# Delta heads: the block inverse in 32-wide quarters with z's projection between its levels, decay distances and four grams moved ahead

## The chip, the cores and the metric

One NeuronCore of a Trainium2 chip runs the whole program. The metric is device time in microseconds of that core for one execution. Engines are named as the profile names them: PE (TensorE; PEld are its weight loads), DVE (VectorE), ACT (ScalarE), POOL (GpSimd), SP (SyncE, which starts DMAs).

## What is computed

The reference is one inference step of a decoder layer: a feed-forward half, differential attention beside a gated DeltaNet branch, a merge, and a second feed-forward half, for 1024 prompt tokens and 32 sample tokens (8 sequences of 4). The change lies in the DeltaNet branch, which per head (8 heads, 128 wide) projects q, k, v and z, convolves and normalizes q, k, v, and then, in chunks, does

```python
decay = jnp.exp(jnp.where(incl, gc[..., :, None] - gc[..., None, :], -jnp.inf))
lower = jnp.where(strict, jnp.einsum('bhncd,bhnmd->bhncm', kb, k) * decay, 0.0)
sol = lax.linalg.triangular_solve(jnp.eye(C) + lower, rhs, left_side=True, lower=True)
qk = jnp.einsum('bhncd,bhnmd->bhncm', q, k) * decay
def step(S, inp):
    v_new = u_i - w_i @ S
    o_i = qd_i @ S + qk_i @ v_new
    S = S * gt_i + kd_i.T @ v_new
o = rmsnorm(o) * silu(z)
```

The kernel computes it with chunks of 128 tokens (8 tiles of the prompt and one of 32 sample rows) and forms the inverse of (I + lower) itself.

## The kernel before

`delta_heads` (L1129) runs eight heads one after another; heads 1 to 5 are a hardware loop (`Fori(1, H - 2)`), the others are written out (`schedule`, L1252). Each engine has its own list of instructions, written by hand, in `head(h)`; they meet only through semaphores (`wait_ge`, `then_inc`), and an engine that waits holds everything behind it in its list. Nothing reorders the lists.

**A projection piece** (`piece`, L1945) is 24 products of 128x128 weights with 352 token columns (8 slices of the 1024 inputs, each as high x high, high x low and low x high parts); c = 0, 1, 2 are the three thirds of the 1056 tokens, and `piece(h, kind, c, i, of)` does part i of `of` of one. Two PSUM banks take turns for them; `take` on ACT empties one. Weights come in by SP (`load`), ACT makes the high part (`high`), DVE the low part (`low`).

**PE's list of a head** (L2018): the last v piece of the head before, with the turns of q and k into token rows (`token`) and the gated output rows of the head before (`out_rows`); q pieces 0 and 1; `grams(0)`, `grams(1)` (products of k with q and k for two tiles each, L2052); q piece 2; `grams(2)`, `grams(3)`; z piece 0, a third of z piece 1, `grams(4)` (the sample tile), the rest of z; then the inverse; then `value_rows`, `key_products`, and the loop over the eight tiles with the state (`fill` puts k and v projections of the next head between the steps).

**The inverse** is built by doubling: the diagonal blocks of size s are inverted, the next level joins pairs of them. For each level 1 to 6 there are, for x = 0, 1 (tiles 0 to 3 and 4 to 7): P = masked lower x U on PE (`pmul`, L2072, into bank 4 + x), a copy to SBUF on ACT (`moves`, L1499), R = turned U x P (`rmul`, L2089, into bank 6 + x), U - R on DVE (`update`, L1767), and the turned U for the next level (`turned`, L1782: DVE turns 32x32 blocks, which suffices below level 6; `tmul` on PE turns the 64-wide blocks at level 6). POOL makes the masked lower for each level (`mask`, L1892). All products of levels 1 to 5 are of whole 128x128 tiles; level 6 is 64x64. Between levels 1, 2, 3 PE does three small steps for the 32 sample rows (L2119, L2122, L2126).

**What feeds it.** The cumulated decay of the head lies in `lo_t` (SP's `load_gc`). DVE makes the distances -|gc_i - gc_j| into `qk_t` (`distances`, L1707, L1709), ACT their exponent into `lo_t` (L1486), POOL the triangle into `qk_t` (L1875, L1877), DVE then multiplies with the grams (`products`, L1717, L1719), POOL masks. POOL's list in a head: kp (L1872), the triangles, the decayed q (L1879, L1881), the masks of level 0, the sample masks (L1903), level 1, kd (L1908), levels 2 to 6, km (L1911).

f32 products appear in the profile as two passes each, a MATMUL and a LDWEIGHTS row for both; the projection's f32r products as one.

Of the kernel before, what the change touches and what calls it, by code (L numbers as in the profile page):

```python
# [7 lines left out]
ALU = mybir.AluOpType  # L8
# [7 lines left out]
P = 128  # L16
# [23 lines left out]
LEVELS = 7  # L40

# [4 lines left out]
C_LEV = C_CAUS + P  # L46
C_ONE = C_LEV + LEVELS * P
# [13 lines left out]
def shape_constants():  # L61
# [6 lines left out]
    for n in range(LEVELS):  # L68
        s = 1 << n
        same = i[:, None] // (2 * s) == i[None, :] // (2 * s)  # L70
        c[:, C_LEV + n * P:C_LEV + (n + 1) * P] = same & (i[:, None] // s % 2 == 1) & (i[None, :] // s % 2 == 0)
# [1057 lines left out]
def delta_heads(nc, m, w_in, w_next, gc_dram, oa_hi_dram, oa_lo_dram, oa_dram, o_dram, state, conv_prompt, conv_sample, delta_prompt, delta_sample):  # L1129
# [6 lines left out]
    with ExitStack() as ctx:  # L1136
# [18 lines left out]

        mask_s, p_mm_s, p_moved_s, t_mm_s, t_moved_s, r_mm_s, u_done_s = (
# [38 lines left out]
        mk = sb("mk", [P, 2, 4, P])  # L1195
        uu = sb("uu", [P, NT, P])
        with ExitStack() as early:
            s_hi, s_lo = (early.enter_context(nc.sbuf_tensor("dl_rows_" + n, [P, H * NS], F32R)) for n in ("hi", "lo"))
        tt = sb("tt", [P, 2, 4, P])
# [5 lines left out]

        ssq = sb("ssq", [P, 4, NT, 2])
# [3 lines left out]
        pp = sb("pp", [P, 2, 4, P])  # L1210
        km = tt[0:NS, :, :, :].rearrange("p a b d -> p (a b) d")
        vn = sb("vn", [P, 2, P])

# [31 lines left out]
        def sample_cols(a):  # L1245

            return a[:, SX:SX + NB * 7].rearrange("p (b w) -> p b w", w=7)

# [43 lines left out]
        def _(sp):  # L1292
# [64 lines left out]
        def _(act):  # L1357
# [83 lines left out]
            def head(h):  # L1441
# [36 lines left out]
                take(h, "q", 0)  # L1478
                take(h, "q", 1)
# [3 lines left out]
                for x in range(3):  # L1483
# [3 lines left out]
                    if x == 0:  # L1487
                        take(h, "q", 2)
# [4 lines left out]
                for c in range(3):  # L1493
                    take(h, "z", c, weights=False)

                def moves(i, x, n):

                    act.wait_ge(p_mm, 12 * h + i + 1)
                    nc.scalar.copy(pp[0:n, x, :, 0:n], bank4(4 + x, 4, n)).then_inc(p_moved, 1)  # L1499
                    if n < P:  # L1500
# [3 lines left out]
                for lev in range(1, LEVELS):  # L1504
                    for x in range(2):
                        moves(2 * (lev - 1) + x, x, P if lev < LAST else P // 2)
                    if lev == 1:
                        n, k = unit(h, "z")
                        if exists(n + 2):
                            high(n + 2, k)  # L1510
                    if lev == 2:
                        act.wait_ge(t_mm_s, h + 1)
                        act.wait_ge(p_mm_s, 2 * h + 2)
                        nc.scalar.copy(pp_s[:, :], m.ps[0:NS, 0, XS:XS + NS]).then_inc(p_moved_s, 1)
# [2612 lines left out]
```

## Time and profile before

| | |
|---|---|
| median of 3 runs | 3486.53 us (3486.32 to 3491.23) |
| profiled execution | 3496.3 us, span 3494.6 us, granted clock 0.99 |
| PE / PEld busy | 3383.1 us (97%) / 3224.6 us (92%) |
| DVE / ACT / POOL busy | 1975.2 us (57%) / 1469.0 us (42%) / 791.7 us (23%) |
| the eight delta heads | 98.7 us each |

Times in the views are us from the span's start. Matmuls are pipelined and their ends are modelled, so the distance between the starts of two of them says more than the length of one; a merged row xN runs from the first start to the last end. The granted clock is that of PE, as a share of 2.4 GHz.

### The profile page before, as it was taken

What the parts mean: (1) busy time and instruction counts of PE and PEld (TensorE: products, weight loads), DVE (VectorE), ACT (ScalarE), POOL (GpSimd) and SP (SyncE); (2) the same over time, 40 slices, a digit from 0 to 9 for tenths busy, and PEclk for the clock granted to TensorE, in tenths of its full rate; (3) what the DMA queues carried; (4) which work ended last, traced back from release to release, by engine and by line L of the source; (5) the groups of instructions that cost most, each with busy time, mean ns of one, the idle gap of its engine ahead of it and who ended that gap; (6) DMA issues with size and microseconds to landing.
All of it is one profiled execution on the core that took longest, in us unless ns stands there. A gap on an engine that the chain in (4) does not pass through costs nothing. (4 is left out here: it accounts for less than half of the span.)

```text
span 3494.6 us, 64138 instructions
## 1 busy us (share of the span) xinstructions
PE 3383.1 (97%) x24746; PEld 3224.6 (92%) x24746; DVE 1975.2 (57%) x3332; ACT 1469.0 (42%) x2993; POOL 791.7 (23%) x644
## 2 busy tenths in 40 slices
PE   7999999999999999898999999999999999999998
PEld 7999999998888888776999999999999899999998
DVE  6655566754555455543566566666341765556555
ACT  5322234545555455433444343444322732223444
POOL 3232210102222221000232334444001332331000
PEclk9999999999999999999999999999999999999999
DMA  4232246732222222499111111114432322224664
GB/s 163 77 87 76 74 153 200 231 107 75 68 68 68 69 68 70 161 356 336 35 51 51 45 38 41 44 45 137 137 99 68 122 76 77 81 82 130 209 191 142
DMA packets 351845, 384.66 MB, mean 110 GB/s; under 512 B 22492, under 2 KB 259110, under 8 KB 351422
## 3 DMA queue, kind: packets, MB, share of 16 engines
q1 hardware_dynamic: 341606, 347.78, 31.7%
q0 software_dynamic: 9888, 32.88, 2.7%
q8 instruction: 179, 2.93, 0.4%
q14 instruction: 88, 0.72, 0.1%
q10 hardware_dynamic: 84, 0.35, 0.0%
HBM read 305.53 MB, written 75.40 MB: 109 GB/s over the span
## 5 line engine op out<-in xcount | busy, mean ns | idle before, releaser
L670 PE MATMUL ps<-p_hi,w_hi 128*128 128x352 f32 x912 | 304.6, 334 | 3.0 <-PEq L120 1.5
L670 PE MATMUL ps<-p_hi,w_lo 128*128 128x352 f32 x912 | 293.7, 322 | 0.0
L670 PE MATMUL ps<-p_lo,w_hi 128*128 128x352 f32 x912 | 293.1, 321 | 0.0
L1960 PE MATMUL ps<-p_hi,w_hi 128*128 128x352 f32 x840 | 281.5, 335 | 3.8 <-DMA p_lo<-d_oa_lo 3.8
L1960 PE MATMUL ps<-p_hi,w_lo 128*128 128x352 f32 x840 | 277.1, 330 | 0.0
L1960 PE MATMUL ps<-p_lo,w_hi 128*128 128x352 f32 x840 | 276.5, 329 | 0.0
L670 PEld LDWEIGHTS ps<-p_hi,w_hi 128*128 128x128 f32 x912 | 172.1, 189 | 5.1 <-issue 1.9
L2773 PE MATMUL ps<-op_hid_hi,w_hi 128*128 128x384 f32 (+1 forms) x528 | 170.9, 324 | 2.7 <-ACT plain L3710 1.7
L2773 PE MATMUL ps<-f_hid_hi,w_hi 128*128 128x352 f32 x528 | 171.3, 324 | 1.5 <-DVE w_lo L2448 1.4
L670 PEld LDWEIGHTS ps<-p_lo,w_hi 128*128 128x128 f32 x912 | 172.5, 189 | 0.0
L670 PEld LDWEIGHTS ps<-p_hi,w_lo 128*128 128x128 f32 x912 | 171.6, 188 | 0.0
L2773 PE MATMUL ps<-f_hid_lo,w_hi 128*128 128x352 f32 x528 | 169.8, 322 | 0.0
L2773 PE MATMUL ps<-f_hid_hi,w_lo 128*128 128x352 f32 x528 | 169.7, 321 | 0.0
L2773 PE MATMUL ps<-op_hid_hi,w_lo 128*128 128x384 f32 (+1 forms) x528 | 169.3, 321 | 0.0
L2773 PE MATMUL ps<-op_hid_lo,w_hi 128*128 128x384 f32 (+1 forms) x528 | 169.3, 321 | 0.0
L1960 PEld LDWEIGHTS ps<-p_hi,w_hi 128*128 128x128 f32 x840 | 159.9, 190 | 5.1 <-issue 3.8
L1960 PEld LDWEIGHTS ps<-p_hi,w_lo 128*128 128x128 f32 x840 | 159.9, 190 | 0.7
L1960 PEld LDWEIGHTS ps<-p_lo,w_hi 128*128 128x128 f32 x840 | 160.1, 191 | 0.5
L1892 POOL TENSOR_TENSOR dl_mk<-dl_lo_t,cst 128x512 f32<-128x512 f32 x112 | 140.9, 1275 | 49.1 <-PE ps L2081 43.1
L2448 DVE TENSOR_TENSOR w_lo<-w_raw,w_hi 128x512 fp32r<-128x512 f32 x136 | 100.5, 746 | 86.6 <-ACT w_hi L2444 86.4
L411 ACT ACTIVATE at_prob<-ps,at_nmax 128x256 f32<-128x256 f32 (+7 forms) x128 | 94.4, 739 | 81.2 <-DVE at_nmax L517 79.5
L2444 ACT CAST w_hi<-w_raw 128x512 fp32r<-128x512 f32 x136 | 83.8, 620 | 105.8 <-PE ps L2773 105.7
(686 smaller groups left out, 10691.6 us busy)
## 6 DMA issues: line engine op xcount, KB each, us to landing
w_raw<-in_ffn_w_out_dram SPq DMA_DIRECT2D x136, 256.0 KB, 3.3
w_raw<-in_w_in_dram SPq DMA_DIRECT2D x67, 512.0 KB, 4.0
sa_v<-in_cache_v_dram SPq DMA_DIRECT2D x120, 256.0 KB, 6.5
w_raw<-in_ffn_w_in_dram SPq DMA_DIRECT2D x48, 512.0 KB, 5.1
sa_k<-in_cache_k_dram SPq DMA_DIRECT2D x72, 256.0 KB, 5.5
f_s<-in_ffn_w_out_dram SPq DMA_DIRECT2D x64, 256.0 KB, 3.3
pair_s<-in_ffn_w_out_dram SPq DMA_DIRECT2D x64, 256.0 KB, 3.2
d_hid<-f_gb SPq DMA_DIRECT2D x44, 264.0 KB, 2.2
```

What stands on the lines that cost most here:

```text
L411: nc.scalar.activation(pr[:, i % 2, a, 0:(i + 1) * P], m.ps[:, 2 + 2 * a:4 + 2 * a, :].rearrange("p b k -> p (b k)")[:, 0:(i + 1) * P], AC ...
L670: mm = nc.tensor.matmul(m.ps[:, bank, 0:CH], a[:, k, w], b[:, f, cols(c)], start=(f == 0 and i == 0), stop=(f == KT - 1 and i == 2))
L1892: nc.gpsimd.tensor_tensor(mk[:, x, :, :], lo_t[:, 4 * x:4 * x + 4, :], msk, ALU.mult).then_inc(mask_done, 1)
L1960: mm = nc.tensor.matmul(m.ps[:, (k + c) % 2, 0:CH], a[:, k, f * P:(f + 1) * P], x[:, f, cols(c)], start=(j == 0), stop=(j == len(terms) - 1))
L2444: nc.scalar.copy(unit_slot(u, False), unit_raw(u)).then_inc(e.out_hi, 1)
L2448: nc.vector.tensor_tensor(unit_slot(u, True), unit_raw(u), unit_slot(u, False).bitcast(F32), ALU.subtract).then_inc(e.out_lo, 1)
L2773: mm = nc.tensor.matmul(m.ps[:, bank, 0:hi - lo], unit_slot(u, low_part)[:, o * P:(o + 1) * P], y[:, k, 0:hi - lo], start=(k == 0 and n == ...
```

## The change

1. Levels 1 to 5 work on 32x32 blocks on the diagonal. POOL cuts the four diagonal blocks of each tile out of `lo_t` into `lo_d` (4 copies of 32 partitions for each x) and makes the masks of levels 0 to 4 at once (`diagonal`). U is kept as `uc` (128 x 32 for each tile). A level is, for each tile and each of four blocks b, one 32x32 product with 32 columns from rows 32b in quarter b. Level 5 joins pairs of blocks straight from `lo_t` (two products for each tile and step). POOL puts the blocks back into the wide `uu` (`put`); level 6 reads `lo_t` itself instead of a mask. `uu` is zeroed once at the start.
2. The last two z pieces are cut into twelve parts of four products, one behind each P and each R step of levels 1 to 5 and two within level 6.
3. On PE, grams(0) to (3) stand ahead of q piece 1, grams(4) ahead of q piece 2.
4. On DVE, `distances` go ahead of the sums and gate rows; ACT takes q's pieces after the exponents; POOL makes kp, decayed q and kd after the masks. SP's `load_gc` waits for p_mm instead of mask_done.
5. Small steps use banks 2 and 3; ACT takes z pieces 1 and 2 behind level 4 and at the end.

The core of the diff:

```diff
-                wait(sp, mask_done, 14 * x)
+                wait(sp, p_mm, 12 * x)
...
                 nc.vector.tensor_scalar(col[:, :, :], m.cols[:, bass.ds(h, 1), :, :].rearrange("p o k t -> p (o k) t"), 1.0, None, ALU.mult).then_inc(staged, 1)
+                dve.wait_ge(staged, h + 1)
+                distances(0)
                 sums(0)
+                distances(1)
+                distances(2)
                 if inner:
...
                 def update(lev, x):
-                    n = P if lev < LAST else P // 2
+                    n = P // 2
+                    tiles = slice(4 * x, 4 * x + 4)
                     dve.wait_ge(r_mm, 12 * h + 2 * (lev - 1) + x + 1)
                     dve.wait_ge(u_done, 14 * h + 2 * (lev - 1) + x + 1)
-                    u = uu[0:n, 4 * x:4 * x + 4, P - n:P]
-                    nc.vector.tensor_tensor(u, u, bank4(6 + x, 4, n), ALU.subtract).then_inc(u_done, 1)
+                    if lev < LAST - 1:
+                        nc.vector.tensor_tensor(uc[:, tiles, :], uc[:, tiles, :], sub4(6 + x), ALU.subtract).then_inc(u_done, 1)
+                    elif lev == LAST - 1:
+                        if isinstance(h, int) and h == 0:
+                            dve.wait_ge(u_zero, 1)
+                        nc.vector.tensor_scalar(uu[0:SUB, tiles, SUB:n], sub4(6 + x)[0:SUB], -1.0, None, ALU.mult)
+                        nc.vector.tensor_scalar(uu[n:n + SUB, tiles, n + SUB:P], sub4(6 + x)[n:n + SUB], -1.0, None, ALU.mult).then_inc(u_done, 1)
+                    else:
+                        nc.vector.tensor_scalar(uu[0:n, tiles, n:P], bank4(6 + x, 4, n), -1.0, None, ALU.mult).then_inc(u_done, 1)
...
+                def diagonal(x):
+                    tiles = slice(4 * x, 4 * x + 4)
+                    pool.wait_ge(low_done, NT * h + 4 * x + 4)
+                    if x == 0:
+                        wait(pool, r_mm, 12 * h)
+                        pool.wait_ge(tri_done, 3 * h + 3)
+                    else:
+                        pool.wait_ge(mask_done, 4 * h + 2)
+                        wait(pool, u_turned, NTURN * h)
+                    pool.nop(nofuse=True)
+                    for b in range(4):
+                        rows = slice(SUB * b, SUB * b + SUB)
+                        nc.gpsimd.tensor_copy(lo_d[rows, tiles, :], lo_t[rows, tiles, rows]).then_inc(cut_done, 1)
+                    pool.wait_ge(cut_done, 8 * h + 4 * x + 4)
+                    first = m.cst[:, C_LEV:C_LEV + SUB].rearrange("p (o d) -> p o d", o=1).to_broadcast([P, 4, SUB])
+                    nc.gpsimd.tensor_tensor(mk[:, x, 0, :, :], lo_d[:, tiles, :], first, ALU.mult).then_inc(mask_done, 1)
+                    k = LEVELS - 3
+                    more_levels = m.cst[:, C_LEV + SUB:C_LEV + SUB + k * SUB].rearrange("p (l o d) -> p l o d", l=k, o=1).to_broadcast([P, k, 4, SUB])
+                    again = lo_d[:, tiles, :].rearrange("p (o t) d -> p o t d", o=1).to_broadcast([P, k, 4, SUB])
+                    nc.gpsimd.tensor_tensor(mk[:, x, 1:1 + k, :, :], again, more_levels, ALU.mult).then_inc(mask_done, 1)
+                def put(x):
+                    tiles = slice(4 * x, 4 * x + 4)
+                    pool.wait_ge(u_done, 14 * h + 2 * (LAST - 2) + x + 1)
+                    if isinstance(h, int) and h == 0 and x == 0:
+                        pool.wait_ge(u_zero, 1)
+                    pool.nop(nofuse=True)
+                    for b in range(4):
+                        rows = slice(SUB * b, SUB * b + SUB)
+                        nc.gpsimd.tensor_copy(uu[rows, tiles, rows], uc[rows, tiles, :]).then_inc(put_done, 1)
...
+                diagonal(0)
+                diagonal(1)
...
+                put(0)
+                put(1)
...
                 piece(h, "q", 0)
-                piece(h, "q", 1)
                 grams(0)
                 grams(1)
-                piece(h, "q", 2)
                 grams(2)
                 grams(3)
+                piece(h, "q", 1)
+                grams(4)
+                piece(h, "q", 2)
                 piece(h, "z", 0)
-                piece(h, "z", 1, 0, 3)
-                grams(4)
-                def pmul(lev, x, n):
-                    pe.wait_ge(mask_done, 14 * h + 2 * lev + x + 1)
...
+                def p_products(lev, x):
+                    if lev == 1:
+                        pe.wait_ge(mask_done, 4 * h + 2 * x + 2)
+                    pe.wait_ge(u_done, 14 * h + 2 * (lev - 1) + x + 1)
+                    if lev > 1:
+                        pe.wait_ge(p_moved, 12 * h + 2 * (lev - 2) + x + 1)
+                    pe.nop(nofuse=True)
                     for j in range(4):
-                        if n < P:
-                            mm = nc.tensor.matmul(m.ps[0:n, 4 + x, j * P:j * P + n], mk[n:P, x, j, 0:n],
-                                                  uu[n:P, 4 * x + j, n:P], start=True, stop=True)
+                        t, out = 4 * x + j, slice(SUB * j, SUB * j + SUB)
+                        if lev < LAST - 1:
+                            for b in range(4):
+                                mm = nc.tensor.matmul(m.ps[rows(b), 4 + x, out], mk[rows(b), x, lev, j, :], uc[rows(b), t, :], start=True, stop=True)
                         else:
-                            mm = nc.tensor.matmul(m.ps[:, 4 + x, j * P:(j + 1) * P], mk[:, x, j, :], uu[:, 4 * x + j, :], start=True, stop=True)
+                            for b in (0, 2):
+                                mm = nc.tensor.matmul(m.ps[rows(b), 4 + x, out], lo_t[rows(b + 1), t, rows(b)], uc[rows(b + 1), t, :], start=True, stop=True)
                     mm.then_inc(p_mm, 1)
...
+                def r_products(lev, x):
+                    pe.wait_ge(p_moved, 12 * h + 2 * (lev - 1) + x + 1)
+                    pe.wait_ge(u_turned, NTURN * h + 2 * (lev - 1) + x + 1)
+                    pe.nop(nofuse=True)
+                    for j in range(4):
+                        t, out = 4 * x + j, slice(SUB * j, SUB * j + SUB)
+                        for b in (range(4) if lev < LAST - 1 else (0, 2)):
+                            mm = nc.tensor.matmul(m.ps[rows(b), 6 + x, out], ttc[rows(b), t, :], ppc[rows(b), t, :], start=True, stop=True)
+                    mm.then_inc(r_mm, 1)
...
+                def p_last(x):
+                    n = P // 2
+                    pe.wait_ge(u_done, 14 * h + 2 * (LAST - 1) + x + 1)
+                    pe.wait_ge(p_moved, 12 * h + 2 * (LAST - 2) + x + 1)
+                    pe.wait_ge(put_done, 8 * h + 4 * x + 4)
...
+                def between(k):
+                    piece(h, "z", 1 + k // 6, k % 6, 6)
+                for lev in range(1, LAST):
                     for x in range(2):
-                        pe.wait_ge(u_done, 14 * h + 2 * (lev - 1) + x + 1)
-                        if lev > 1:
-                            pe.wait_ge(p_moved, 12 * h + 2 * (lev - 2) + x + 1)
-                        pmul(lev, x, n)
-                        if lev == LAST:
-                            tmul(x, n)
+                        p_products(lev, x)
+                    between(2 * lev - 2)
                     for x in range(2):
-                        rmul(lev, x, n)
+                        r_products(lev, x)
                     if lev == 1:
...
+                    between(2 * lev - 1)
+                pe.wait_ge(u_done_s, 2 * h + 2)
+                p_last(0)
+                p_last(1)
+                between(10)
+                between(11)
+                r_last(0)
+                r_last(1)
+                pe.wait_ge(taken, 3 * unit(h, "z")[0] + 3)
```

## Rows read from the trace of the kernel before

**Rows 1.** An inner head: length, busy us of PE, PEld, DVE, ACT, POOL, then clock, DMA.

```profile
1895.57:1994.28 98.71, 97.45 (x685) 93.17 (x684) 61.75 (x106) 41.19 (x106) 36.81 (x29) 0.97 0.15 44
```

**Rows 2.** Timeline of PE, the inverse: start, us, engine, line, operation, [idle before].

```profile
1930.02 1.95 PE L2081 MATMUL ps<-dl_uu,dl_mk 128*128 128x128 f32 x16
...
1934.71 2.39 PE L2081 MATMUL ps<-dl_uu,dl_mk 128*128 128x128 f32 x16 [0.70 <-POOL dl_mk L1892]
...
1951.23 0.65 PE L2078 MATMUL ps<-dl_uu,dl_mk 64*64 64x64 f32 x8
...
1954.25 1.76 PE L2138 MATMUL ps<-cst,dl_cs 128*128 128x128 f32 x8
```

**Rows 3.** Timeline of PE: passes on 32 columns, sample attention and a small step.

```profile
1493.69 1.06 PE L1079 MATMUL ps<-vals,w_raw 128*32 128x128 f32 x32
...
1496.77 0.24 PE L1051 MATMUL ps<-k_s,sa_q_zeroed 128*32 128x32 f32 x8
...
1939.06 0.24 PE L2123 MATMUL ps<-dl_uu,dl_mk_s 32*32 32x32 f32 x2
```

**Rows 4.** Groups of PE by line and shape: busy us, mean ns of one.

```profile
L1079 PE MATMUL ps<-vals,w_raw 128*32 128x128 f32 x64 | 2.0, 274 | 0.0
...
L1051 PE MATMUL ps<-k_s,sa_q_zeroed 128*32 128x32 f32 x8 | 0.2, 194 | 0.0
...
L2078 PE MATMUL ps<-dl_uu,dl_mk 64*64 64x64 f32 x16 | 1.3, 222 | 0.1
```

**Rows 5.** Timeline of PE, a change of tile shape and back.

```profile
1922.93 0.32 PE L1960 MATMUL ps<-p_hi,w_hi 128*128 128x352 f32 x1
1923.09 0.32 PE L1960 MATMUL ps<-p_lo,w_hi 128*128 128x352 f32 x1
1923.33 0.30 PE L2052 MATMUL ps<-dl_css 128*32 128x64 f32 x2
1923.56 0.43 PE L1960 MATMUL ps<-p_hi,w_lo 128*128 128x352 f32 x1
```

**Rows 6.** Timeline of ACT, the copy of a level.

```profile
1931.11 0.59 ACT L1499 COPY dl_pp<-ps 128x512 f32<-128x512 f32 x1 [0.43 <-PE ps L2081]
```

**Rows 7.** Timeline of DVE, distances and products.

```profile
1908.56 2.60 DVE L1707 TENSOR_TENSOR dl_qk_t<-dl_lo_t,dl_col 128x512 f32<-128x512 f32 x1
...
1911.81 0.68 DVE L1707 TENSOR_TENSOR dl_qk_t<-dl_lo_t,dl_col 128x512 f32<-128x512 f32 x1
...
1917.19 0.35 DVE L1717 SCALAR_TENSOR_TENSOR dl_lo_t<-ps,dl_sc,dl_lo_t 128x128 f32<-128x128 f32 x1
...
1917.65 0.34 DVE L1717 SCALAR_TENSOR_TENSOR dl_lo_t<-ps,dl_sc,dl_lo_t 128x128 f32<-128x128 f32 x1
```

**Rows 8.** Timeline of ACT, the exponents.

```profile
1911.53 1.28 ACT L1481 ACT_TABLE_LOAD   x1
...
1914.02 0.63 ACT L1486 ACTIVATE dl_lo_t<-dl_qk_t 128x512 f32<-128x512 f32 x1
```

**Rows 9.** Timeline of POOL, triangles and a mask.

```profile
1914.72 2.16 POOL L1875 TENSOR_TENSOR dl_qk_t<-dl_lo_t,cst 128x512 f32<-128x512 f32 x1 [4.11 <-ACT dl_lo_t L1486]
...
1919.92 1.29 POOL L1877 TENSOR_TENSOR dl_qk_t<-dl_lo_t,cst 32x32 f32<-32x32 f32 x1
...
1927.11 1.28 POOL L1892 TENSOR_TENSOR dl_mk<-dl_lo_t,cst 128x512 f32<-128x512 f32 x1
```

**Rows 10.** Timeline of POOL, a copy of 32 partitions in attention.

```profile
903.81 0.28 POOL L600 COPY v_s<-at_v_rows 32x128 f32<-32x128 f32 x1 [7.25 <-DVE at_o_lo L561]
```

**Rows 11.** Busy times of one stretch, columns as in rows 1.

```profile
1964.70:1968.20 3.50, 3.50 (x15) 3.50 (x15) 0.10 (x1) 0.27 (x1) 0.00 (x0) 0.51 0.00 0
```

**Rows 12.** Timeline of PE ahead of that stretch and in it.

```profile
1961.61 1.85 PE L2200 MATMUL ps<-dl_wq,dl_sts 128*128 128x8 f32 x16
...
1965.22 0.49 PE L1960 MATMUL ps<-p_hi,w_lo 128*128 128x352 f32 x1
1965.51 0.49 PE L1960 MATMUL ps<-p_hi,w_hi 128*128 128x352 f32 x1
```

More of the change, by code:

```diff
@@ L1486, in head @@
                     nc.scalar.activation(lo_t[0:n, 4 * x:4 * x + k, 0:n], qk_t[0:n, 4 * x:4 * x + k, 0:n], ACT.Exp).then_inc(decay_done, 1)
-                    if x == 0:
-                        take(h, "q", 2)
+                for c in range(3):
+                    take(h, "q", c)
                 if not more:
@@ L1492, in head, with moves @@
                     nc.scalar.activation(zs[:, :], xc[:, 0, 0:T], ACT.Silu).then_inc(z_silu, 1)
[L1493 to L1499, printed above, removed]
-                    if n < P:
+                take(h, "z", 0, weights=False)
+                def moves(lev, x):
+                    act.wait_ge(p_mm, 12 * h + 2 * (lev - 1) + x + 1)
+                    if lev < LAST:
+                        nc.scalar.copy(ppc[:, 4 * x:4 * x + 4, :], sub4(4 + x)).then_inc(p_moved, 1)
+                    else:
+                        n = P // 2
+                        nc.scalar.copy(pp[:, x, :, :], bank4(4 + x, 4, n)).then_inc(p_moved, 1)
                         act.wait_ge(t_mm, 2 * h + x + 1)
@@ L1737, in head @@
                 low(n, k)
-                if not more:
-                    row_low(0)
-                    row_low(1)
-                for x in range(3):
-                    distances(x)
-                    if x == 1:
-                        gather(h, 2)
-                        product(h, 2, 1)
-                if not more:
-                    row_low(2)
+                gather(h, 2)
+                product(h, 2, 1)
                 for t in range(NT):
                     products(t)
-                    if t == 3:
-                        product(h, 2, 2)
+                    if not more and t == 3:
+                        row_low(0)
+                if not more:
+                    row_low(1)
                 def base(x):
@@ new lines, in head @@
+                diagonal(0)
+                diagonal(1)
+                pool.wait_ge(low_done, NT * h + NT)
+                wait(pool, p_mm_s, 2 * h)
+                for i in range(2):
+                    nc.gpsimd.tensor_tensor(mk_s[:, i, :], lo_t[0:NS, TT, 0:NS], m.cst[0:NS, C_LEV + i * SUB:C_LEV + i * SUB + NS], ALU.mult).then_inc(mask_s, 1)
+                pool.wait_ge(scales, 4 * h + 4)
+                nc.gpsimd.tensor_tensor(kp[:, :, :], tok[:, :, 1, :], by_scale(BPE), ALU.mult).then_inc(kp_done, 1)
@@ new lines, in p_last @@
+                def p_last(x):
+                    n = P // 2
+                    pe.wait_ge(u_done, 14 * h + 2 * (LAST - 1) + x + 1)
+                    pe.wait_ge(p_moved, 12 * h + 2 * (LAST - 2) + x + 1)
+                    pe.wait_ge(put_done, 8 * h + 4 * x + 4)
+                    pe.nop(nofuse=True)
+                    for j in range(4):
+                        mm = nc.tensor.matmul(m.ps[0:n, 4 + x, j * P:j * P + n], lo_t[n:P, 4 * x + j, 0:n], uu[n:P, 4 * x + j, n:P], start=True, stop=True)
+                    mm.then_inc(p_mm, 1)
```

132 lines of the change are left out of this document (60 added, 72 removed).

## Prediction

> **What bounds the kernel now.** I read the page first. Section 1, engines by busy time, has PE far ahead of DVE. So what counts is how long PE needs for its own list and where it waits. The slices show the granted clock at nine tenths or more throughout. Next, the busy times by stretch: in one inner head of the delta loop (1895.57 to 1994.28, 98.71 us; eight such heads in the kernel) PE is busy for 97.45 us, DVE for 61.75, POOL for 36.81 [rows 1]. An edit that only shifts work to another engine brings nothing here; one that shortens PE's list brings it nearly whole.
>
> Then PE's timeline of that head. The levels of the inverse run as one block, with no other product between them. L2081 (P) and L2097 (R) alternate, 16 passes each, the first P at 1930.02, the second at 1934.71, five pairs, until the last level's 64-wide products start at 1951.23 and value_rows at 1954.25 [rows 2]. Levels 1 to 5 take 21.2 us, level 6 takes 3.0, together 24.2 us. A phase of 16 passes is about 1.95 us with its last pass's 0.28, so some 0.11 a pass. PE's 0.70 us of waiting ahead of level 2 is put down to POOL's mask [rows 2]. The z projection stands ahead of the block, where it hides the chain that feeds the first mask.
>
> **Packing, levels 1 to 5.** A phase of 16 full passes (two for each of 8 tiles) becomes 64 passes of 32x32 with 32 columns in levels 1 to 4, and 32 passes in level 5: 576 passes a head in place of 160. What they cost depends on whether quarters run side by side. The trace has each half of this: L1079 uses four column quarters, and 32 passes of 128 columns fill 1.06 us of which one pass is 0.27, so 0.79/31 = 0.025 us a pass, against the 0.11 of the whole array; L1051, with 32 columns, has eight passes in 0.24 us where one is 0.194, so they start 0.007 apart [rows 3, 4]. With the last pass of a group, four side by side, costing what one costs, I need the pitch of one quarter: 64x64 passes with 64 columns fill 0.65 us by eights, one being 0.222, so 0.061 apart [rows 2, 4]; half the columns, near 0.028. The four starts of a group at 0.007 come to 0.028 too. A tile, two passes in each of four quarters, is then 0.056 us and a phase 8 x 0.056 = 0.45 us. Upper bound of the overlapped case: passes of one quarter lie 0.045 apart (L2123: two 32x32 passes in 0.24 us [rows 3], one of them as long as L1051's), a phase 0.75 us. I take 0.45, since the eight of L2078 show that passes behind the first come closer.
>
> **The change of shape.** The z pieces put whole-array products on either side of each phase, so PE changes tile shape twice. L1960 to the 32-column L2052 is 1923.09 to 1923.33, 0.24 us against the 0.16 from one L1960 to the next, so +0.08; back, the two passes of L2052 and the way to L1960 take 0.23 together, some +0.12 [rows 5]. A phase costs 0.45 + 0.08 + 0.12 = 0.65 us, ten of them 6.5. The three small 32x32 steps behind levels 1 to 3 stay, now within the same shape: 0.3 together. Levels 1 to 5: 6.8 us in place of 21.2. Level 6 keeps its matrices; it gets two pieces in the middle, one more pair of shape changes and a small one at its start: 3.0 + 0.3 = 3.3 us. The block is 10.1 us in place of 24.2: **14.1 us less a head**.
>
> **Is the chain within a level covered?** Between P and R, and between R and the next P, stands a piece of four z products, 4 x 0.16 = 0.64 us, with the two changes of shape 0.85 or so. P to R: ACT starts 0.3 us after P's last start, and each copy has a quarter of the columns: I estimate half of L1499's 0.59 or less [rows 6], two of them 0.6. R of tiles 0 to 3 needs the first only. R to P: DVE's update shrinks in the same way, two are 0.6 to 0.7; the turns shrink too and are wanted only by the next R. About 0.85 us against 0.85: covered, with little to spare; if it isn't, 0.2 us at ten places is 2 us a head. ACT's silus stand behind the copies of level 5, ahead of those of level 6, as now; PE then has an R, a piece and a P to do. POOL's masks, which the 0.70 us waited for, are made ahead of level 1, so that wait goes.
>
> **The work moved ahead.** z's last two thirds (48 x 0.16 = 7.7 us) no longer hide what comes before the first P. Without waits PE would come there at 1930.02 - 7.7 = 1922.3. I follow the feeding chain, head start unchanged. DVE now starts distances(0) at 1908.56 and is at distances(1) at 1911.81; L1707 takes 2.60 us for the first beside POOL's kp, 0.68 alone [rows 7]. Moved ahead of the sums, with kp behind the masks, the three cost 3.1 us in place of 5.1, part of it in gaps where DVE waits for ACT's squares. So the sums end near 1908.2, scales, low, gather and one product near 1913.3. ACT's exponentials now need the root ahead of them, and that the last sums: table load at 1908.5, and as now 3.1 us from it (1911.53) to the end of the first decay (1914.02 + 0.63) [rows 8]: 1911.6. POOL's triangle product, 1.28 alone for this shape (L1892) to 2.16 beside DVE, gives 1913.0 to 1913.9 [rows 9]. DVE's products, 0.46 us a tile (1917.19 to 1917.65) [rows 7], begin then. PE: q0 (24 x 0.16) to 1907.0, four grams 3.1 and q1 3.85, so 1913.9; grams(4), now ahead of q2, wait for the first two tiles' products, 1914.9: **a new wait of about 1 us**, with q2 and z0 queued behind it. DVE ends tile 7 at 1917.7. POOL's diagonal(0) needs tile 3 (1915.8) and triangle three: four copies at 0.28 (L600 copies 32x128 in that), a mask at 0.4, one at 1.28; twice, 5.6 to 6 us in all, ends near 1922 [rows 9, 10]. PE arrives at 1923.3. So P waits 0 to 1 us. One of DVE's 1080-column products lies between the two turns, on the way of the second half. New waits together 0.6 to 2.6 us, taken 1.6: **12.5 us less a head**. kp, q and kd behind the masks on POOL, three operations of 1024 or 1152 columns, each under 3.2 us at L1892's rate of 0.0025 a column and its start, end by 1932; put needs level 4, which ends near 1934, copies 2 x 1.1, and p_last comes at 1937: free. take(z,2) runs under r_last. Behind put on POOL wait km and the DMAs of the tails, not wanted before the states. SP's load_gc waits for p_last's products instead of the last mask; only the next head's loads queue behind it, and lo_t is wanted at the next distances, the whole state loop later.
>
> **The sum.** 8 x 12.5 = 100 us. The profiled execution is 3496.3 us (span 3494.6), 9.8 above the median of the runs; it gives 3396, the median 3486.5 gives **3386**. Own range of this case: new waits 0.6 instead of 1.6, and one late fall of the clock less a head in three, 3486.5 - 8 x 13.6 - 6 = 3372, less 10 for a stage that is shorter than its rows add up to: 3362; phases of 0.75 us (3.0 a head) and waits of 2.6, 3486.5 - 8 x 8.5 = 3418.
>
> **Rivals.** (1) *The quarters come in turn.* No row has passes that differ in both row and column quarter and write the same bank. If they start one behind another, 0.028 apart, a phase of 64 is 1.8 us: 8 x 1.35 + 2 x 0.45 = 11.7 back of 12.5, hence 3480. Where they do overlap but PE can't be fed faster than the 0.025 us a pass that L1079 sustains (the 0.007 of L1051 is a burst of eight), a phase of 64 is 1.6 us and of 32 0.8: 8 x 1.15 + 2 x 0.35 = 9.9 back, 3466. Middle 3473.
> The Trainium skill speaks against the change here: TensorEngine Tiling (Array Packing), Restrictions and Gotchas, says that different row tiles can't use one PSUM bank at the same time. Here all four write bank 4 + x or 6 + x, though in different partitions. TensorE: Matmul & The Clock Gate, section "Wait — 56ns, not 53.3ns?", gives about 62 ns for a MATMUL when the sequencer's firmware decodes it; 288 x 62 would be 17.9 us a head and the time 3494, an estimate from that page. L1079's 16 products (32 passes) in 1.06 us are 0.05 to 0.07 each and refute neither.
> (2) *Slower: in turn, with the load exposed, and the clock falls.* At 0.045 a pass 576 passes are 25.9 us against 4.5, 21.4 back of 12.5: 8.9 us worse a head, 3558. The turning point is (4.5 + 12.5)/576 = 0.030 us a pass. An emptier array brings the other part: from 1964.7 to 1968.2, behind an array fed little by 16 passes of 8 columns, the granted clock is 0.51, the level of 1.2 GHz, and L1960 starts every 0.29 us instead of 0.16 [rows 11, 12]. If all twelve pieces ran so, +6.2 us a head. In the forecast nearly half of each level is z at full width, so I expect no more falls than now.
> (3) *POOL is late.* L1877, a 32x32 operation, took 1.29 us beside DVE's convolution [rows 9]. At that price diagonal ends 8 us later and the eight copies of put bind too: some 2.6 us left of 12.5, 3466.
> (4) *No change*: rival 1 at its worst, or two of these in part.
>
> **Chances.** Forecast 0.70, rival 1 0.10 (a fifth of it within the bound of no change), rival 2 0.10, rival 3 0.05, rival 4 0.05. The range takes in the first, rival 3 and most of rival 1: 3362 to 3478. About 0.2%, 7 us, is what a measurement of this kernel can tell from none. Faster 0.83, same 0.07, slower 0.10.
>
> **What would show it.** Right: P and R phases of 64 passes with 0.45 us from first to last start; PE waits ahead of grams(4) and of the first P of 0 to 2 us, none elsewhere in the block; ten pieces of four z products; p_last some 14 us behind the first P; a head near 86 us; clock 0.97 or more. Wrong: phases of 1.8 us (rival 1), 3 us with a clock near 0.5 (rival 2), or PE waiting for POOL's dl_mk or dl_uu by microseconds (rival 3).

## The result and the profile after

| | before | after |
|---|---|---|
| median of 20 runs each, same chip | 3491.88 us (3486.32 to 3501.72) | 3483.47 us (3476.24 to 3492.07) |
| ratio after / before, 95% interval | | 0.9972 (0.9964 to 0.9979) |
| profiled execution, span | 3494.6 us | 3478.1 us |

One run after, of 12249.86 us at a granted clock of 0.57, is left out of the range and of the ratio.

The change makes the kernel 0.28% faster, about 8 us (the two profiled executions happen to lie 16.5 us apart). The prediction was 3386 us, with 3478 as its upper end: of the 100 us forecast nine tenths are missing.

The page of the kernel after, engines by busy time and the instruction queue (packets, MB, share):

```profile
span 3478.1 us, 70910 instructions
...
PE 3326.4 (96%) x28074; PEld 3147.3 (90%) x28074; DVE 1932.1 (56%) x3348; ACT 1440.9 (41%) x2993; POOL 700.9 (20%) x693
...
q8 instruction: 236, 3.87, 0.5%
```

PE's busy time fell by 57 us (from 3383.1), but the span by 16.5 only. The other 40 us are idle time of PE that was not there before. The waits of PE in the delta stage (1690 to 2400) name it; the columns are us in total, times, longest:

```profile
PE ps L2131 <- DVE dl_uc L1779: 34.7, 7, 5.1
PE ps L2004 <- issue: 9.3, 5, 2.5
PE ps L2131 <- DVE dl_uc L1770: 2.9, 6, 0.6
```

L2131 is P, L2145 is R, L2004 is the projection's product (L1960 before), L1779 is DVE's update, L1770 the base. Seven times PE stands 5 us ahead of level 2's P. The timelines of DVE and POOL in one head show why; they answer to [rows 7] and [rows 9]:

```profile
1918.62 0.31 DVE L1770 STREAM_TRANSPOSE dl_uc<-dl_ttc 128x128 f32<-128x128 f32 x1
1918.86 7.84 DVE L1608 SCALAR_TENSOR_TENSOR dl_cs<-dl_xc,conv_weight,dl_cs 128x1080 f32<-128x1080 f32 x1
1926.62 0.47 DVE L1779 TENSOR_TENSOR dl_uc<-dl_uc,ps 128x128 f32<-128x128 f32 x2
...
1918.87 2.10 POOL L1939 TENSOR_TENSOR dl_kp<-dl_tok,dl_sc 128x1152 f32<-128x1152 f32 x1
1920.94 2.34 POOL L1941 TENSOR_TENSOR dl_q_t<-dl_q_t,dl_cs 128x1024 f32<-128x1024 f32 x1
1923.24 0.24 POOL L1943 TENSOR_TENSOR dl_wq<-dl_q_t,dl_css 128x32 f32<-128x32 f32 x1
1923.45 2.10 POOL L1948 TENSOR_TENSOR dl_kd<-dl_tok,dl_col 128x1152 f32<-128x1152 f32 x1
```

`product(h, 2, 3)`, a convolution product of 1080 columns, and kp start within 0.01 us of each other. The product ends 7.84 us later, 1.15 us after the last of POOL's four operations; by itself it takes 1.33 us (e2 below). It takes 7.83 to 7.85 us in all eight heads. Level 1's update is queued behind it on DVE. PE's timeline of the same head, against [rows 2], and the busy times of the stretch behind (length, PE, PEld, DVE, ACT, POOL, clock, DMA):

```profile
1918.17 0.45 PE L2131 MATMUL ps<-dl_uc,dl_mk 32*32 32x32 f32 x32
1919.08 0.45 PE L2131 MATMUL ps<-dl_uc,dl_mk 32*32 32x32 f32 x32 [0.45 <-DVE dl_uc L1770]
...
1920.30 0.86 PE L2145 MATMUL ps<-dl_lo_d,dl_ttc 32*32 32x32 f32 x64
...
1927.04 1.08 PE L2131 MATMUL ps<-dl_uc,dl_mk 32*32 32x32 f32 x64 [4.91 <-DVE dl_uc L1779]
...
1936.62 0.77 PE L2131 MATMUL ps<-dl_uc,dl_mk 32*32 32x32 f32 x64
...
1928.00:1934.80 6.80, 6.80 (x154) 5.44 (x143) 0.99 (x4) 1.07 (x6) 0.00 (x0) 0.51 0.01 2
```

Behind the 4.91 us the granted clock is 0.51, the level of 1.2 GHz, for about 10 us in nearly every head; before, the stage had seven falls, each of 3.4 us.

For the rest I measured each head between first passes on PE's timeline, the mean of heads 1 to 5. T is the first token transpose, P the first P of the block, V the first of value_rows (before, P to V is the block of 24.2 us and the 7.7 us of z pieces ahead of it that are now inside). V to T is the stretch that leads into the head, from the V of the head before:

| us | T to P | P to V | V to T | head |
|---|---|---|---|---|
| before | 25.6 | 31.9 | 39.3 | 96.8 |
| predicted change | +1.6 | -14.1 | 0 | -12.5 |
| after | 25.6 | 29.4 | 41.3 | 96.3 |
| e1 | 25.9 | 24.4 | 40.4 | 90.8 |
| e2 | 26.0 | 23.9 | 40.1 | 89.9 |
| e6 | 26.3 | 23.8 | 39.3 | 89.3 |
| e7 | 26.3 | 20.0 | 39.0 | 85.3 |
| e8 | 34.0 | 22.1 | 40.9 | 96.9 |
| e9 | 26.3 | 26.3 | 40.0 | 92.6 |
| e10 | 25.6 | 24.3 | 43.4 | 93.3 |

The table ahead of the change gives 98.7 us for each of the eight heads before. That is the length of two of the heads 1 to 5; the other three take 95.5, and the two longer ones hold two falls of the clock of 3.4 us each.

### The profile page after: what moved, and what is told of

The parts are those of the page before. It is cut to its first block and busy times, and to the rows that moved or that the text cites. A ratio compares the mean times of both kernels' runs of the same rounds, so it can differ in the third digit from the quotient of the medians.

```text
span 3478.1 us, 70910 instructions
## 1 busy us (share of the span) xinstructions
PE 3326.4 (96%) x28074; PEld 3147.3 (90%) x28074; DVE 1932.1 (56%) x3348; ACT 1440.9 (41%) x2993; POOL 700.9 (20%) x693
## 5 line engine op out<-in xcount | busy, mean ns | idle before, releaser
L673 PE MATMUL ps<-p_hi,w_hi 128*128 128x352 f32 x912 | 304.8, 334 | 2.6 <-PEq L123 1.4
L2004 PE MATMUL ps<-p_hi,w_hi 128*128 128x352 f32 x840 | 290.7, 346 | 9.1 <-issue 9.0
L673 PE MATMUL ps<-p_hi,w_lo 128*128 128x352 f32 x912 | 293.6, 322 | 0.0
L673 PE MATMUL ps<-p_lo,w_hi 128*128 128x352 f32 x912 | 293.2, 321 | 0.0
L2004 PE MATMUL ps<-p_lo,w_hi 128*128 128x352 f32 x840 | 286.6, 341 | 0.0
L2004 PE MATMUL ps<-p_hi,w_lo 128*128 128x352 f32 x840 | 286.2, 341 | 0.2 <-issue 0.2
L2004 PEld LDWEIGHTS ps<-p_hi,w_hi 128*128 128x128 f32 x840 | 164.8, 196 | 12.5 <-issue 9.8
L2004 PEld LDWEIGHTS ps<-p_lo,w_hi 128*128 128x128 f32 x840 | 164.9, 196 | 2.1
L2004 PEld LDWEIGHTS ps<-p_hi,w_lo 128*128 128x128 f32 x840 | 165.1, 197 | 1.8 <-issue 0.5
L1608 DVE SCALAR_TENSOR_TENSOR dl_cs<-dl_xc,conv_weight,dl_cs 128x1080 f32<-128x1080 f32 x72 | 153.9, 2138 | 4.4 <-DVE dl_cs L1603 2.1
```

The costliest lines, as they stand in the source:

```text
L673: mm = nc.tensor.matmul(m.ps[:, bank, 0:CH], a[:, k, w], b[:, f, cols(c)], start=(f == 0 and i == 0), stop=(f == KT - 1 and i == 2))
L1608: nc.vector.scalar_tensor_tensor(out=cs[:, u, 0:CO], in0=xc[:, u, i:i + CO], scalar=wgt[:, i:i + 1], in1=cs[:, u, 0:CO], op0=ALU.mult, op1 ...
L2004: mm = nc.tensor.matmul(m.ps[:, (k + c) % 2, 0:CH], a[:, k, f * P:(f + 1) * P], x[:, f, cols(c)], start=(j == 0), stop=(j == len(terms) - 1))
```

## The experiments

**e1, the product later.** Takes the convolution product off the way of level 1's update.

```
                 base(1)
-                product(h, 2, 3)
...
                     if lev == 3:
+                        product(h, 2, 3)
                         dve.wait_ge(r_mm_s, h + 1)
```

> The changed kernel with one step of DVE's list moved: the last product of v's convolution, product(h, 2, 3), from ahead of level 1's update to behind level 3's turns. Theory A (POOL's kp, q, kd, four operations back to back, hold up this SBUF-only DVE operation, 7.84 us instead of 1.34; level 1's update stands behind it in DVE's list, and PE waits 4.9 us and then runs 10 us at a clock of 0.5): the wait ahead of level 2 falls to under 0.5 us, the clock inside the block stays at 1.0, a head goes from 96 to about 88.5 us, the time to 3420 to 3430. Rival B (the sparse array of the 32x32 passes is what lowers the clock): the wait goes, but PE still runs at 0.5 for some 10 us of each block, a head near 91.5, the time near 3450. Rival C (another wait takes its place, the copies or updates within a level being late): waits of 0.3 us or more at several phases, the time above 3455.

Measured: 3450.78 us, ratio 0.9889 (0.9868 to 0.9909). Level 2's wait is gone from the waits of PE. In its place stand, in the same view, many short ones without a named releaser:

```profile
PE ps L2004 <- issue: 13.7, 10, 2.5
PE ps L2145 <- issue: 9.4, 17, 1.0
```

Of theory A the wait and the clock came true: between P and V the granted clock is 1.00 in heads 1 to 5, where the changed kernel has 0.78 to 0.88. So rival B is out, though the time is the one that it named. The time missed theory A's 3420 to 3430 us by 20. No theory had the idle time without a releaser, which grew from 9.8 us in the changed kernel to 25.3.

**e2, POOL waits.** The other side of the same collision: the order on DVE stays, POOL starts kp only when the product is done.

```
                 pool.wait_ge(scales, 4 * h + 4)
+                pool.wait_ge(conv_done, 12 * h + 12)
                 nc.gpsimd.tensor_tensor(kp[:, :, :], ...)
```

> The changed kernel with DVE's list as it is; only POOL waits ahead of kp until that last product is done (a wait on conv_done). Theory A: the product takes 1.34 us again, PE's wait ahead of level 2 is under 0.5 us, and kp, q, kd end 1.5 us later than now, which nobody waits for: the time within 0.2% of e1_product_later, 3420 to 3430. If it was the place of the product in DVE's list and not POOL's operations beside it that made it long, it stays at 7.8 us and the time at 3480.

Measured: 3439.62 us, ratio 0.986 (0.9839 to 0.988). DVE's timeline has the same two operations as above:

```profile
1906.17 1.33 DVE L1608 SCALAR_TENSOR_TENSOR dl_cs<-dl_xc,conv_weight,dl_cs 128x1080 f32<-128x1080 f32 x1
1908.25 0.67 DVE L1779 TENSOR_TENSOR dl_uc<-dl_uc,ps 128x128 f32<-128x128 f32 x2 [0.75 <-PE ps L2146]
```

One line on POOL, with no operation added, moved between engines or left out, takes some 40 us off the changed kernel (0.9972 less 0.986, of 3491 us, is 39; the medians say 44). It is the concurrence of the two that cost, not the work of either: in e1 and e2 both are still done. The time is 10 us above the range expected; idle time without a releaser is 21.9 us here.

**e3 and e4, written out.** The changed kernel's PE stands 2.0 to 2.5 us at four head boundaries, each time at the loop's jump back, and at none of the boundaries outside the loop:

```profile
1987.70 0.42 PE L2004 MATMUL ps<-p_hi,w_hi 128*128 128x352 f32 x1 [2.03 <-issue]
```

e3 is e1 with heads 1 to 5 one after another; e4 does the same to the kernel before.

```
-            with eng.Fori(1, H - 2) as h:
+            for h in range(1, H - 1):
                 head(h)
-            head(H - 2)
             head(H - 1)
```

> e1_product_later with heads 1 to 5 written out instead of the hardware loop, nothing else. Theory D (the 2.0 to 2.5 us PE stands still at four of the head boundaries, and not at the others, belong to the loop's jump back: PE's part of the body has grown and its instructions are not there in time): these four gaps go, 9 us less than e1_product_later. Rival (the gaps are a data wait at a head's start): they stay, the same time as e1_product_later.

> The kernel before with heads 1 to 5 written out. Its trace has no gap at the jump back, so theory D expects no change, within 0.2%; if writing out is worth something by itself, here too, it shows as the same 9 us.

Measured: e3 3447.3 us (3435.96 to 3448.35), 3.5 under e1 with overlapping intervals; e4 3493.8, ratio 1.0007 (0.9995 to 1.0019). The gaps at the jump are gone in e3, and the kernel before never had them. The time hardly follows: in V to T, where the gap lay, a fall of the clock of 3.4 us takes its place in two of e3's heads 1 to 5 and in four of e6's (39.6 us from V to T there, 38.0 where there is neither gap nor fall). e3's profiled execution, span 3434.3 us, is at the low end of its runs.

**e6, both repairs.** e2's line and e3's heads.

> Both repairs: GpSimd waits for the head's last convolution product before kp, q and kd (as in e2_pool_waits), and heads 1 to 5 are written out one after another instead of looping (as in e3_written_out). Theory: the two costs lie in different places, so they add. The loop's jump back left TensorE idle 2.2 to 2.6 us at four head boundaries in e2's trace, 9 us in all; off e2's 3439.6 us that is about 3431 us, 3424 to 3436, ratio to the kernel before about 0.983. Rival: the idle time at the jump is not lost but taken up elsewhere (instruction supply is limited as a whole, and e3's median was only 3.5 us under e1's), then it stays at 3437 to 3442 us with more short idle stretches inside the levels.

Measured: 3438.69 us, ratio 0.985 (0.9834 to 0.9867): the rival of that expectation. Against e2 nothing is gained. PE's timeline of one head, P and R of levels 1 to 4:

```profile
1907.44 0.75 PE L2145 MATMUL ps<-dl_lo_d,dl_ttc 32*32 32x32 f32 x64
1909.64 0.75 PE L2131 MATMUL ps<-dl_uc,dl_mk 32*32 32x32 f32 x64 [0.30 <-issue]
1911.15 0.70 PE L2145 MATMUL ps<-dl_lo_d,dl_ttc 32*32 32x32 f32 x58
1913.17 0.26 PE L2145 MATMUL ps<-dl_lo_d,dl_ttc 32*32 32x32 f32 x6 [1.31 <-issue]
1914.27 0.75 PE L2131 MATMUL ps<-dl_uc,dl_mk 32*32 32x32 f32 x64
1915.80 0.60 PE L2145 MATMUL ps<-dl_lo_d,dl_ttc 32*32 32x32 f32 x46
1917.45 0.37 PE L2145 MATMUL ps<-dl_lo_d,dl_ttc 32*32 32x32 f32 x18 [1.05 <-issue]
```

A pause in the middle of a phase, behind its 58th or 46th pass, can be no semaphore: the waits stand ahead of its first and its 33rd pass. I counted PE's passes from one such pause to the next, in e3, e6 and e8: where two follow closely it is 125 or 126 nearly every time. The next three runs ask what that is.

**e7, half the products.** Two of the four blocks of each tile.

```
-                            for b in range(4):
+                            for b in (0, 2):
...
-                        for b in (range(4) if lev < LAST - 1 else (0, 2)):
+                        for b in (0, 2):
```

> e6 with two of the four blocks of 32 left out of each tile in levels 1 to 4, so 32 passes a phase instead of 64; half of the inverse's small levels is not computed. Theory that the passes are limited by their issue (about 0.009 us each, whichever quarter they go to, and with it the supply of instructions): a phase falls from 0.58 to about 0.29 us, eight phases of the four levels give 2.3 us a head, and the short idle stretches without a wait (about 2 us a head in e2's and e3's traces) mostly go as well: 25 to 35 us less than e6, about 3400 us. Theory that each quarter of the array is the limit (16 passes one after another in each of four): a phase stays at 0.55 to 0.6 us, and the time stays within 5 us of e6. Theory that the chain through ScalarE and VectorE sets the pace of a level: phases get shorter, but idle time with a named wait (ScalarE's copy, VectorE's update) takes their place, and the time falls by under 10 us.

Measured: 3418.97 us, ratio 0.9789 (0.9773 to 0.9806), 20 under e6. The kernel leaves out half of the work of levels 1 to 4, so it only tells of time. The waits without a releaser in the blocks of all heads fall from 18.6 us (L2145 9.3, L2131 8.9, level 5's 0.4) to 2.0. In the profiled execution the last head loses again: P to V at a granted clock of 0.56 takes 38.4 us, against 32.1 at 0.79 in e6. But a phase of 32 passes is no half of one of 64:

```profile
1907.59 0.69 PE L2131 MATMUL ps<-dl_uc,dl_mk 32*32 32x32 f32 x32
1909.05 0.69 PE L2145 MATMUL ps<-dl_lo_d,dl_ttc 32*32 32x32 f32 x32
```

With the last pass's 0.19 that is 0.50 us from first to last start, against 0.75 - 0.19 = 0.56 for 64. So a phase is set by the 16 passes of one quarter, about 0.03 us each, and most of the saving is the pauses: the first theory had the pauses right and the second the phase. The page also gives the size of a transfer: e7 has 65537 instructions and 211 packets on q8, e6 69633 and 227. That is 4096 instructions for 16 packets, 256 in one, four to a product (a load and a matmul for either pass). 125 to 126 passes with their loads, 250 to 252 instructions, are then about one packet.

**e8, z ahead.** The pieces leave the levels.

```
                 piece(h, "z", 0)
+                piece(h, "z", 1)
+                piece(h, "z", 2)
...
                 def between(k):
-                    piece(h, "z", 1 + k // 6, k % 6, 6)
+                    return
```

> e6 with z's parts 1 and 2 whole ahead of the levels instead of in twelve pieces between their phases: TensorE has nothing to do between the phases. Theory: the pieces hide the chain product, copy, product, update, turn of each level. Exposed, a level costs two phases of 0.6 us and the chain's 1.5 to 2 us beside them, where the pieces now take 1.9 us a level: 6 to 12 us a head are lost, 50 to 100 us in all, and the granted clock falls in the levels: 3480 to 3540 us. Rival: the interleaving itself is what costs (two changes of shape a phase, and instructions of two kinds to be supplied), and the chain is short: then e8 stands within 15 us of e6, on either side.

Measured: 3500.69 us, ratio 1.0023 (1.0014 to 1.0033), 62 over e6. As large as the theory said, and the clock falls as it said, but the chain has little part in it. PE's timeline, levels 1 to 4, and the busy times of that block from P to V:

```profile
1933.89 0.75 PE L2147 MATMUL ps<-dl_lo_d,dl_ttc 32*32 32x32 f32 x64 [0.19 <-ACT dl_lo_d L1506]
...
1935.78 0.54 PE L2147 MATMUL ps<-dl_lo_d,dl_ttc 32*32 32x32 f32 x36 [0.18 <-ACT dl_lo_d L1506]
1937.56 0.44 PE L2147 MATMUL ps<-dl_lo_d,dl_ttc 32*32 32x32 f32 x28 [1.24 <-issue]
...
1941.37 0.78 PE L2147 MATMUL ps<-dl_lo_d,dl_ttc 32*32 32x32 f32 x33 [1.86 <-issue]
...
1945.86 0.78 PE L2147 MATMUL ps<-dl_lo_d,dl_ttc 32*32 32x32 f32 x38 [2.05 <-issue]
...
1932.95:1954.18 21.23, 15.27 (x624) 13.37 (x623) 7.01 (x26) 7.11 (x21) 3.24 (x9) 0.66 0.08 22
```

The bare chain costs 0.19 us a phase; the two tile groups x = 0 and 1 cover each other. The pauses cost 1.2 to 2.1 us each, 3.8 and 4.5 us apart. P to V takes 22.1 us without any piece, and took 23.8 with twelve of them, 11.5 us with their changes of shape, inside. Two things fill the room of the pieces. The idle time without a releaser grows from 2.3 us a head (18.6 in eight) to 5.6 (39.3 in the seven that the view holds), so about 3.3 us of the pieces' time lay where PE would wait for instructions. And the granted clock between P and V is 0.58 to 0.66 in all heads, where e6 has 1.00 in five, 0.93 in two and 0.79 in the last: the block without full-width products runs mostly at half the clock.

**e9, quarter by quarter.** The same products in another order.

```
-                    for j in range(4):
-                        for b in range(4):
+                    for b in range(4):
+                        for j in range(4):
```

> e6 with the same products in another order: all four of a quarter one after another, then the next quarter, instead of the four quarters in turn for each tile. Theory that passes are limited by their issue and a quarter has room: no change, phases 0.58 us, within 4 us of e6. Theory that the quarters' work overlaps only where neighbours in the order go to different quarters: a phase grows from 0.58 us toward the time of 64 passes of 32 columns in turn, by 0.3 to 0.9 us; eight phases in a head make that 2.4 to 7 us a head, 20 to 55 us in all: 3450 to 3485 us.

Measured: 3484.95 us, ratio 0.998 (0.9958 to 1.0003), 46 over e6. Its phases:

```profile
1933.59 1.51 PE L2130 MATMUL ps<-dl_uc,dl_mk 32*32 32x32 f32 x64
1935.86 1.51 PE L2144 MATMUL ps<-dl_lo_d,dl_ttc 32*32 32x32 f32 x64
```

1.32 us from first to last start in place of 0.56, for the same products into the same banks: neighbours in the order have to go to different quarters. With the slower phases the pauses are gone (0.2 us in all): a level now takes 4.8 us, and a packet's worth of passes lasts longer than the pace of the packets. The order by itself costs 2.5 us a head (26.3 against 23.8), 20 of the 46 us. Most of the rest lies in the profiled execution's first and last head, whose blocks ran at a granted clock of 0.64 and 0.56 and took 37.1 and 46.5 us, 14 more than in e6 each; the first:

```profile
1731.74:1768.81 37.07, 37.07 (x671) 32.14 (x671) 8.92 (x29) 7.68 (x22) 9.67 (x15) 0.64 0.11 31
```

**e10 and e11, the pieces elsewhere.** e10 is e2 with all twelve pieces in levels 1 to 4. e11 is e10 with ScalarE's take of z part 0 in the last head behind level 2's copies.

```
                 def between(k):
-                    piece(h, "z", 1 + k // 6, k % 6, 6)
+                    first = (0, 1, 2, 3, 5, 7, 9, 11, 12, 12, 12, 12, 12)
+                    for i in range(first[k], first[k + 1]):
+                        piece(h, "z", 1 + i // 6, i % 6, 6)
```

> e2_pool_waits with z's twelve pieces all between the phases of levels 1 to 4, where the 64-pass phases stand (1, 1, 1, 2, 2, 2, 2, 1 pieces), and none in levels 5 and 6. Theory that TensorE waits for instructions (125 or 126 passes apart, about one in 4.1 us, in e3, e6 and e8): the four levels take at least 4.1 us each by the supply whatever stands in them, so up to 2 us a head of pieces lies in time that was lost; against it stand some 0.2 us for each of four phases in levels 5 and 6 whose chain is now bare (0.18 us in e8): 0.8 to 1.5 us a head gained, 7 to 12 us in all, 3427 to 3433 us. Theory that the pieces are needed to cover the chain: levels 5 and 6 lose 1 to 2 us a head, 8 to 16 us in all, 3448 to 3456 us, and the idle stretches without a wait stay as they are.

> e10 with one more edit: in the last head ScalarE takes z's first part (whose buffer GpSimd's q product must have left) behind level 2's copies instead of ahead of level 1's. Expected: the wait of 5.4 us of the last head's first R phase for ScalarE's copy goes, and the stretch at half the clock behind it (13.7 us in e6's trace) with it: 5 to 11 us less than e10. Rival: the waiting only passes to TensorE's z part 2 or to GpSimd's end of the head, then within 2 us of e10.

Measured: e10 3465.12 us, ratio 0.992 (0.9906 to 0.9933), some 20 slower than e2 by the ratios, where I expected 10 less; e11 3462.41, 0.9907 (0.9892 to 0.9922), not to be told from e10. The pauses did shrink (L2146, L2132 and level 6 together from 9.1 to 4.7 us), and the bare chain in levels 5 and 6 costs little (waits for the copies and updates there are 4.2 us in all). What I had not counted, busy times of two stretches of e10 show:

```profile
1937.67 0.94 PE L2146 MATMUL ps<-dl_lo_d,dl_ttc 32*32 32x32 f32 x32 [0.29 <-ACT dl_lo_d L1507]
1939.06 0.76 PE L2156 MATMUL ps<-dl_uu,dl_lo_t 64*64 64x64 f32 x8 [0.45 <-DVE dl_uu L1784]
...
1939.60:1946.40 6.80, 6.80 (x47) 6.10 (x47) 3.37 (x7) 2.75 (x6) 1.89 (x1) 0.51 0.50 155
1953.20:1956.60 3.40, 3.40 (x14) 3.40 (x14) 0.68 (x1) 0.47 (x3) 0.00 (x0) 0.51 0.00 0
```

Behind levels 5 and 6 without full-width products the granted clock falls to 0.51 for 6.8 us, and again for 3.4 us, in most heads. P to V is 24.3 us, near e2's 23.9; the 3.3 us a head are lost in V to T (43.4 against 40.1). Both theories missed: the z pieces in levels 5 and 6 hide little of the chain, they keep the array full ahead of the long products.

e11's wait also moved instead of going: PE's 5.4 us for ScalarE's copy in the last head became 4.4 us without a releaser at the small transposition behind level 2.

## Why the prediction was wrong, by its steps

**The step that failed first** is "kp, q and kd behind the masks on POOL ... free". It checked only when they end (by 1932 predicted, 1925.6 measured) against who wants them, not what DVE does meanwhile. Two things were at hand. The row for it: L1707 takes 2.60 us beside POOL's kp and 0.68 alone [rows 7]; the text used this row for the gain of moving kp away and not for the price where kp goes. And DVE's list: between base(1) and level 1's update stands `product(h, 2, 3)`, which the text never names; it has only "one of DVE's 1080-column products" between the two turns. The chain "about 0.85 us against 0.85: covered" was right for every level but the first, whose update had 7.84 us ahead of it. Price: P to V 29.4 us in place of 23.9 (e2), V to T 1.2 us more; some 40 us in all (e2). It is paid in the wait and in the stretch at half the clock behind it.

The Trainium skill has the rule: SBUF — State Buffer, in "Who interferes with whom", says that a VectorE operation with two SBUF inputs and a GpSimd operation that reads SBUF exclude each other, and the second to start is blocked until the first has finished. The trace agrees in kind and differs in two points: by the recorded starts the one held was the first to start, by 0.01 us, and it wasn't let in between POOL's four operations either, and paid for all of them (7.84 us).

**The supply of instructions** was in no step and is what stands between e2 and the forecast. Halving the passes took 3.8 us a head off P to V (e6 to e7). The shorter phases are 8 x 0.06 = 0.5 of it, idle time without a releaser 2.1 ((18.6 - 2.0)/8). The last 1.2 us aren't placed; one fall of the clock of 3.4 us in one of e6's five blocks can account for 0.3. In the kernel after the pauses hardly show (0.5 us at L2131): the late update gives the supply time to catch up, and the pieces at half the clock take longer. That is argued, not tried. Rival 1 named a feeding limit, but as the spacing within a phase; the spacing is 0.009 us a pass there, and the limit bites only over a whole packet. About 4 us for a packet of 126 passes or 63 products is 0.064 us a product, 0.032 a pass. A phase of 32 products in 0.56 us runs at 0.018 each, so the pace is no floor for each product, and the pauses stand at packet lengths, also where z's single-pass products are among the 126. TensorE: Matmul & The Clock Gate, "Wait — 56ns, not 53.3ns?", in the Trainium skill, has about 62 ns a MATMUL for decoding by firmware. No run here shows that pace: by the packet count a pass is an instruction pair of its own, so a MATMUL takes 0.032 us in the long run, about half of that figure. The prediction set the 62 ns against products (288 x 62) where the passes are 576; L1079's passes, 0.025 us apart [rows 3], spoke against it already.

**The phases** were mis-sized: 0.56 to 0.58 us from first to last start, not 0.45 (0.036 us a pass of one quarter, where 0.028 was taken between bounds of 0.45 and 0.75). The piece with its two changes of shape (a piece is four z products) is 0.96 us (1907.59 to 1909.05 in e7, less 0.50), not 0.84. e7's 20.0 us from P to V against 31.9 - 14.1 = 17.8 predicted are ten phases at 0.05 more, ten pieces at 0.12 more, and the 0.3 to 0.5 us ahead of the second half of the first P: 2.1 of 2.2.

**What held.** The quarters overlap, so the heart of rival 1 and rival 2 fell, e9 against e6 shows it. The rule on which rival 1 leaned, that row tiles can't use one PSUM bank at once (the Trainium skill, TensorEngine Tiling (Array Packing), Restrictions and Gotchas), doesn't hold for this case: four quarters that differ in rows and columns write one bank side by side, 64 passes in 0.56 us. No run has quarters that differ in rows alone. The work moved ahead cost nothing: T to P is 25.6 us before and after with z's two thirds gone from it, waits of 0.45 us at the second half of the first P and of up to 0.9 at grams(4) in three heads, where 1.6 was taken. POOL's masks and put were on time, so rival 3 fell too.

**The sum as measured**, on the 17.8 us from P to V: 2.2 for phases and shapes, 3.8 for supply and 64 instead of 32 passes (23.8, e6), 0.1 to e2, 5.5 for the collision (29.4). In V to T there are 2.0 us more than before, from the clock and the loop's jump; in T to P 1.6 less than predicted. 5.5 + 3.8 + 0.1 + 2.2 + 2.0 - 1.6 = 12.0 of the 12.5.

**What stays open.** That the pauses come from the instruction supply rests on their spacing, on e7, where they go with the number of instructions, and on e9, where they go with slower phases. A fourth sign is in e6's trace: from 1901 to 1928 PE pauses five times without a releaser (1902.46, 1906.03, 1909.64, 1913.17, 1917.45), and five instruction packets are moved:

```profile
q8 instruction: 5, 0.08, 1.1%
```

1.1% of 27 us on 16 engines is 0.95 us for a packet. What in the supply takes 4 us for it wasn't tried.

No run was made either on why a jump back costs 2 us in the changed kernel and nothing in the one before, but the same queue tells them apart. From 1900 to 2180, within the loop's turns, the kernel before moves no instruction packet on q8 at all, and the kernel after moves these:

```profile
q8 instruction: 31, 0.51, 0.8%
```

Written out, the kernel before moves 16 there (e4). So before, PE's part of the loop wasn't brought in again from one turn to the next, and in the changed kernel it is, in every turn. A turn of PE's list has about 1370 rows before (685 and 684 in [rows 1]) and about 2200 after. That the longer list no longer fits into what PE keeps is the reading at hand; no run varies the length alone.

The best versions are e2 and e6, at 3439 us both; e2 needs one line.

## What to carry to other kernels

When an operation is moved on one engine, lay it beside the lists of the engines that it can hold up or that can hold it up, not only beside the time at which its result is wanted, and read in each list what stands behind the operation that it can hold up. When products are made smaller, count instructions over a few microseconds as well as passes in a phase, and see in the page whether a loop's instructions are brought in again in every turn. Work that is put between small products may be worth its place by keeping the clock or bridging the supply, and moving it to where the chain is longest can cost more than it covers.

## What the hardware showed that I had not expected

- A DVE product of 1.33 us took 7.84 us beside four POOL operations in a row (2.10, 2.34, 0.24, 2.10 us), although it had started 0.01 us ahead of the first.
- Quarters of the array with different rows and columns run side by side into one bank: 64 passes of 32x32 in 0.56 us by turns, in 1.32 us quarter by quarter. 32 passes in two quarters took 0.50.
- PE's stream of small products paused by 0.2 to 2.4 us. Where two pauses followed closely they were 125 or 126 passes apart, about one packet of 256 instructions, and 3.5 to 4.6 us.
- The jump back of a loop left PE idle for 2.0 to 2.6 us in the kernels with packed levels, whose turns brought in some 11 instruction packets each, and not in the one before, whose later turns brought in none.
- Levels of small products alone ran at a granted clock of 0.58 to 0.66 (e8), with full-width pieces between them at 1.00 in most heads (e6).
